# Three model blocks on one core: middle layers' projections as three fp32r products, attention outputs as halves three heads later, constants multiplied in TensorE's waits

## The reference, cut to what matters

```python
# second block, layer 0                       # layer 1
x = x + 0.5 * swiglu(rms_norm(x), ...)         # the same
proj = rms_norm(x) @ ab_w_in    # 1024x1536    # proj = rms_norm(x) @ c_w_in  (q k v 3072, index 512+64+8)
y = cat(pool_mixer(u), conv_module(a, gate))   # y = dsa_attention(...): 16 heads of 64
x = x + y @ ab_w_out            # 1024x1024    # x = x + y @ c_w_out
x = x + 0.5 * swiglu(rms_norm(x), ...)         # the same
# third block: swiglu, layer_norm; then
proj = h @ w_in ; y_ssm = mamba2_branch(z, xbc, dt) @ w_ssm_out
y_att = moba_attention(q, k, v) @ w_att_out    # 8 heads of 128
x = layer_norm(a*h + (g_ssm * y_ssm + g_att * y_att) @ w_o) ; then swiglu, layer_norm
```

## Time and profile before

| what | us |
|---|---|
| median of 3 executions | 3916.43 |
| the profiled execution | 3912.03 |
| its span, first to last instruction | 3910.2 |
| TensorE busy in it | 3252.5 (83%) |
| VectorE busy | 2156.8 (55%) |
| ScalarE busy | 1014.4 (26%) |
| mean granted TensorE clock | 0.952 of full |

### The profile page before, as it was taken

How to read it: one execution, slowest core, us unless ns; L and a number is a source line. 1 busy time by engine, 2 the same in 40 slices (tenths; PEclk the granted TensorE clock), 3 DMA queues, 4 the chain that set the end, 5 groups by cost and what they waited for, 6 DMA issues and landing times. The chain is left out here.

```text
span 3910.2 us, 34931 instructions
## 1 busy us (share of the span) xinstructions
PE 3252.5 (83%) x12416; PEld 2229.5 (57%) x12416; DVE 2156.8 (55%) x3737; ACT 1014.4 (26%) x1597; POOL 1033.1 (26%) x1092
## 2 busy tenths in 40 slices
PE   5897567778887577777998999999998989878798
PEld 3673222223664222223876687876687878767686
DVE  5578766544559766645544455523445435555654
ACT  0211111111112111112432344412343312434333
POOL 0027777764016777764000000000000000200000
PEclk9799899999899899999998999998999989989999
DMA  9369999999549999999651455542455534243453
GB/s 365 142 226 368 409 409 409 409 404 369 229 152 344 409 409 409 409 409 338 195 167 65 157 187 168 187 146 86 130 185 173 185 124 147 75 154 128 151 183 118
DMA packets 402041, 951.19 MB, mean 243 GB/s; under 512 B 30652, under 2 KB 171488, under 8 KB 401632
## 3 DMA queue, kind: packets, MB, share of 16 engines
q0 software_dynamic: 147456, 536.94, 34.9%
q1 hardware_dynamic: 245088, 397.09, 30.3%
q10 hardware_dynamic: 9344, 15.22, 1.1%
HBM read 948.06 MB, written 1.07 MB: 243 GB/s over the span
## 5 line engine op out<-in xcount | busy, mean ns | idle before, releaser
L1463 PE MATMUL PS<-v_rows,xn 128*128 128x512 f32 x1944 | 910.4, 612 | 360.9 <-DMA v_rows<-in_peer_v_dram,peer_ids 350.8
L1463 PEld LDWEIGHTS PS<-v_rows,xn 128*128 128x128 f32 x1944 | 356.4, 193 | 913.8 <-issue 553.6
L1544 DVE CUSTOM_DVE_ANT_0 u_rows<-u_rows,PS 128x1024 f32<-128x1024 f32 x512 | 621.8, 1220 | 365.9 <-DMA u_rows<-in_peer_u_dram,peer_ids 338.1
L760 DVE TENSOR_TENSOR ring_lo<-ring,ring_hi 128x2048 fp32r<-128x2048 f32 x198 | 452.9, 2292 | 260.3 <-ACT ring_hi L699 259.8
L1618 POOL DMA_INDIRECT u_rows<-in_peer_u_dram,peer_ids x512 | 484.7, 947 | 268.9 <-issue 145.2
L1618 POOL DMA_INDIRECT v_rows<-in_peer_v_dram,peer_ids x512 | 487.5, 952 | 169.3 <-issue 144.3
L699 ACT CAST ring_hi<-ring 128x2048 fp32r<-128x2048 f32 x198 | 376.7, 1912 | 287.1 <-PE PS L616 156.2
L616 PE MATMUL PS<-ring_hi,hT_hi 128*128 128x512 f32 x1056 | 420.2, 398 | 16.6 <-DVE hT_lo L800 12.1
L616 PE MATMUL PS<-ring_hi,hT_lo 128*128 128x512 f32 x1056 | 414.3, 392 | 0.0
L616 PE MATMUL PS<-ring_lo,hT_hi 128*128 128x512 f32 x1056 | 413.8, 392 | 0.0
L442 PE MATMUL PS<-hT,ring 128*128 128x256 f32 x1664 | 366.9, 382 | 1.2 <-DVE hT L406 1.2
(11 more groups left out here) (400 smaller groups left out, 3708.3 us busy)
## 6 DMA issues: line engine op xcount, KB each, us to landing
ring<-in_ffn_w_gate_dram SPq DMA_DIRECT2D x132, 512.0 KB, 3.9
ring<-in_ffn_w_up_dram SPq DMA_DIRECT2D x132, 512.0 KB, 4.9
ring<-in_ffn_w_down_dram SPq DMA_DIRECT2D x66, 1024.0 KB, 4.8
ring<-in_w_in_dram SPq DMA_DIRECT2D x64, 1024.0 KB, 5.1
ada_ring<-in_ada_w_dram SPq DMA_DIRECT2D x96, 512.0 KB, 8.6
ring<-in_peer_wq_dram SPq DMA_DIRECT2D x16, 1024.0 KB, 7.3
ring<-in_c_w_in_dram SPq DMA_DIRECT2D x14, 1024.0 KB, 5.0
ring<-in_w_out_dram SPq DMA_DIRECT2D x8, 1024.0 KB, 12.2
```

What stands on the lines that cost most here:

```text
L760: nc.vector.tensor_tensor(halves(c)[1], slot, halves(c)[0], ALU.subtract).then_inc(S.w_lo, 1)
L1463: ins = nc.tensor.matmul(self.PS[:, 2 * b + h, :], diag[:, r % NDIAG, :], rowsV[:, m % VRING, h * BANK:(h + 1) * BANK], start=(n % (slots ...
L1544: ins = nc.vector.tensor_tensor_reduce(rowsU[:, m % URING, :], rowsU[:, m % URING, :], H[b], 1.0, 0.0, ALU.mult, ALU.add, dots[:, e:e + 1])
```

## The change

1. `ab_in`, `ab_out`, `c_in` (but for its narrow job) and `c_out` go through `project_halves`. New `tokens_hi` and `tokens_lo` split `hT`; `self.plain` names chunks that aren't split; `output_projection` takes halves and the number of chunks prepared by the stage before.
2. Kind "F" is three products of 256 columns in every place; outputs lie in two banks, and the additions behind the old form (L2447 and L2478, and their like for the keys) go away.
3. `attention` writes its output as halves: ScalarE rounds head h-2 after it has copied the transposed weights of head h, VectorE subtracts head h-3 at the beginning of its step h. The later split in `att_out` goes away.
4. `norm_vector` does what it had between (a `weights_lo`) ahead of the wait for GpSimd's power.
5. `keep_clock` multiplies two constant 128x128 tiles into a PSUM bank that nobody reads, `count` times, at 28 places of the code.

```diff
+    def keep_clock(self, bank, count):
+        for _ in range(count):
+            self.nc.tensor.matmul(self.PS[:, bank, 0:P], self.ones, self.ident, start=True, stop=True, skip_group_check=True)
-    def norm_tensor(self, pe, S, src=None):
+    def norm_tensor(self, pe, S, src=None, lead=17, pause=4):
+        self.keep_clock(2, lead)
...
+        self.keep_clock(2, pause)
@@ norm_vector
         nc.vector.drain().then_inc(S.n_ms, 1)
+        if between:
+            between()
         ve.wait_ge(S.n_rstd, 1)
...
-        if between:
-            between()
+    def tokens_hi(self, act, S, hh):
+        act.drain()
+        for g in range(2):
+            if g == 1:
+                act.wait_ge(S.n_hT, self.N_HT)
+            self.nc.scalar.copy(hh[:, 4 * g:4 * g + 4, 0, :], self.hT[:, 4 * g:4 * g + 4, :]).then_inc(S.h_hi, 1)
+    def tokens_lo(self, ve, S, hh):
+        ve.drain()
+        for g in range(2):
+            ve.wait_ge(S.h_hi, g + 1)
+            self.nc.vector.tensor_tensor(hh[:, 4 * g:4 * g + 4, 1, :], self.hT[:, 4 * g:4 * g + 4, :], hh[:, 4 * g:4 * g + 4, 0, :],
+                                         ALU.subtract).then_inc(S.h_lo, 1)
@@ project_halves, kind "F"
-                            out, col = self.PS[:, quad + t, :], slice(t * P, (t + 1) * P)
-                            nc.tensor.matmul(out, w_hi[:, kk, col], both[:, k, :], start=st, stop=False, skip_group_check=True)
-                            ins = nc.tensor.matmul(out[:, 0:SEQ], w_lo[:, kk, col], tok_hi[:, k, :], start=False, stop=sp,
+                            out, col = self.PS[:, pair + t // 2, (t % 2) * SEQ:(t % 2 + 1) * SEQ], slice(t * P, (t + 1) * P)
+                            nc.tensor.matmul(out, w_hi[:, kk, col], tok_hi[:, k, :], start=(st and t % 2 == 0), stop=False, skip_group_check=True)
+                            nc.tensor.matmul(out, w_hi[:, kk, col], tok_lo[:, k, :], start=False, stop=False, skip_group_check=True)
+                            ins = nc.tensor.matmul(out, w_lo[:, kk, col], tok_hi[:, k, :], start=False, stop=sp, skip_group_check=True)
@@ ab_in, tensor and vector
-                    self.norm_tensor(pe, S)
-                    pe.wait_ge(S.n_hT, self.N_HT)
-                    self.project(pe, S, [("F", 512)] * 3, self.hT, KT)
+                    self.norm_tensor(pe, S, lead=23, pause=11)
+                    self.project_halves(pe, S, ["F"] * 3, hh[:, :, 0, :], hh[:, :, 1, :], KT, ready=S.h_lo)
+                    self.keep_clock(7, 9)
...
+                    self.norm_vector(ve, S, gain, None, lambda: self.weights_lo(ve, S, 0, 1))
+                    self.tokens_lo(ve, S, hh)
+                    self.weights_lo(ve, S, 1, 2)
@@ attention, vector
+            def out_lo(h):
+                ve.wait_ge(S.a_hi, h + 1)
+                nc.vector.tensor_tensor(YT_lo[rows(h), h // per, :], self.PS[rows(h), 4 + h % 2, 0:SEQ], YT_hi[rows(h), h // per, :],
+                                        ALU.subtract).then_inc(S.a_out, 1)
...
             for h in range(heads):
+                if h >= 3:
+                    out_lo(h - 3)
                 if h + 2 < heads:
                     masked(h + 2)
                 normalised(h)
-                if h >= 2:
-                    self.attention_out(ve, S, nc.vector.tensor_copy, h - 2, rows, per, YT)
@@ attention, scalar
+            def out_hi(h):
+                act.wait_ge(S.a_val, h + 1)
+                nc.scalar.copy(YT_hi[rows(h), h // per, :], self.PS[rows(h), 4 + h % 2, 0:SEQ]).then_inc(S.a_hi, 1)
...
                     exponentials(h + 1)
                 turned(h)
+                if h >= 2:
+                    out_hi(h - 2)
@@ c_in, scalar
+                    self.weights_hi(act, S, 4, 8)
                     for h in range(8):
                         act.wait_ge(S.index, h + 1)
...
                     for j in (3, 5, 7):
+                        self.weights_hi(act, S, 2 * j + 2, 2 * j + 6 if j < 7 else 2 * j + 3)
                         self.leave(act, j)
@@ c_in, vector
+                    self.weights_lo(ve, S, 6, 8)
                     evacuate(2)
@@ conv stage, the new ends of scalar and vector
+                    for c in (0, 2):
+                        nc.scalar.copy(YT_hi[:, 4 + c:6 + c, :], YT[:, 4 + c:6 + c, :]).then_inc(S.y_hi, 1)
...
+                    for i, c in enumerate((slice(0, 4), slice(4, 6), slice(6, 8))):
+                        ve.wait_ge(S.y_hi, i + 1)
+                        nc.vector.tensor_tensor(YT_lo[:, c, :], YT[:, c, :], YT_hi[:, c, :], ALU.subtract)
```

More of the change, by code:

```diff
@@ L480, in project_halves @@
                 if n >= self.base + self.ahead:
-                    pe.wait_ge(S.w_lo, n - self.base - self.ahead + 1)
+                    pe.wait_ge(S.w_lo, self.halves_made(n))
+                if ready is not None and j == first:
+                    pe.wait_ge(ready, g + 1)
                 w_hi, w_lo = [ring[:, n % self.half_slots, :].rearrange("p (k n) -> p k n", k=4)
@@ L580, in _, with ffn @@
                 self.sum_columns(self.PS[:, 0, KT:2 * KT], 1).then_inc(S.columns, 1)
-    def ffn(self, name, gain=None, layer_norm=None):
+                self.keep_clock(1, 14)
+    def ffn(self, name, gain=None, layer_norm=None, after=4):
         nc = self.nc
@@ L1814, in _, with output_projection, attention @@
                     nc.gpsimd.tensor_tensor(self.rstd[:], self.ms[:], self.neghalf[:, 0:NB], ALU.pow).then_inc(S.c_rstd, 1)
-            self.output_projection("ab_out", YT)
-    def output_projection(self, name, YT):
-        with self.stage("p_free0 p_free1", name) as (block, S):
+            self.output_projection("ab_out", YT_hi, YT_lo, 2)
+    def output_projection(self, name, YT_hi, YT_lo, ahead):
+        self.ahead = ahead
+        with self.stage("p_free0 p_free1 w_hi w_lo", name) as (block, S):
             @block.tensor
             def _(pe):
-                self.project(pe, S, [("T", 512)] * 2, YT, KT)
+                self.project_halves(pe, S, ["T"] * 2, YT_hi, YT_lo, KT)
+            @block.scalar
+            def _(act):
+                self.weights_hi(act, S, self.ahead, 4)
             @block.vector
             def _(ve):
+                self.weights_lo(ve, S, self.ahead, 4)
                 self.plain_residual(ve, S)
-    def attention(self, block, S, ctx, heads, dh, QT, KT_, V, mask, bias, YT):
+    def attention(self, block, S, ctx, heads, dh, QT, KT_, V, mask, bias, YT_hi, YT_lo):
         nc = self.nc
@@ L1917, in _ @@
                 normalised(h)
-                if h >= 2:
-                    self.attention_out(ve, S, nc.vector.tensor_copy, h - 2, rows, per, YT)
-            for h in (heads - 2, heads - 1):
-                self.attention_out(ve, S, nc.vector.tensor_copy, h, rows, per, YT)
+            for h in range(heads - 3, heads):
+                out_lo(h)
         @block.scalar
@@ L1942, in _ @@
                 turned(h)
-    ATT = "a_scores a_masked a_max a_exp a_norm a_turn a_turned a_val a_out"
-    def attention_out(self, eng, S, copy, h, rows, per, YT):
-        eng.wait_ge(S.a_val, h + 1)
-        copy(YT[rows(h), h // per, :], self.PS[rows(h), 4 + h % 2, 0:SEQ]).then_inc(S.a_out, 1)
+                if h >= 2:
+                    out_hi(h - 2)
+            for h in (heads - 2, heads - 1):
+                out_hi(h)
+    ATT = "a_scores a_masked a_max a_exp a_norm a_turn a_turned a_val a_hi a_out"
     def sparse_attention(self):
@@ L2100, in _ @@
                     pe.wait_ge(side, 48)
-                self.attention(block, S, ctx, AH, 64, QT, KT_, V, mask[:], B, YT)
-            self.output_projection("c_out", YT)
+                self.attention(block, S, ctx, AH, 64, QT, KT_, V, mask[:], B, YT_hi, YT_lo)
+            self.output_projection("c_out", YT_hi, YT_lo, 1)
     def turn_plain(self, pe, S, src):
@@ L2401, in mamba @@
         self.place_halves(ctx, 2)
-        both = hh[:].rearrange("p k i n -> p k (i n)")
         YT_hi = self.sb("ssm_yT_hi", [P, 16, SEQ], F32R, ctx=ctx)
         YT_lo = self.sb("ssm_yT_lo", [P, 16, SEQ], F32R, ctx=ctx)
-        with ExitStack() as inner, self.stage("p_free0 p_free1 w_hi w_lo z z_used q_lo g_ms g_rstd g_y turned scaled out_hi out_lo", "ssm_z") as (block, S):
+        with ExitStack() as inner, self.stage("p_free0 p_free1 w_hi w_lo z z_used g_ms g_rstd g_y turned scaled out_hi out_lo", "ssm_z") as (block, S):
             Z = self.gate[:].rearrange("p i (b n) -> p i b n", b=NB)
@@ L2578, in moba @@
         pre = self.xn[:].rearrange("p i (b n) -> p i b n", b=NB)
-        YT_hi = self.sb("moba_yT_hi", [P, KT, SEQ], F32R, ctx=ctx)
-        YT_lo = self.sb("moba_yT_lo", [P, KT, SEQ], F32R, ctx=ctx)
-        with self.stage("p_free0 p_free1 w_hi w_lo y_hi y_lo pre sig", "att_out") as (block, S):
+        with self.stage("p_free0 p_free1 w_hi w_lo pre sig", "att_out") as (block, S):
             def gate(i):
```

197 lines of the change are left out of this document (123 added, 74 removed).

## The result

The changed kernel takes 3898.51 us (median of 8 runs, 3886.48 to 3907.61) against 3920.66 us (3915.93 to 3930.78, 8 runs) before: ratio 0.9939, 95% interval 0.9921 to 0.9958, some 22 us. I had forecast 78.7 and a range that ends at 3878. The direction was right and the size wrong by a factor of three and a half. The profiled execution took 3892.48 us.

What follows compares the result with a forecast made beforehand. Outside the peer stages TensorE was taken as the bound, by its products and by half-clock stretches after waits. -43.7 - 2 + 18.2 + 23.1 - 2.8 - 71.5 = -78.7 us from 3916.4 gave 3838, range 3808 to 3878.

Steps and rivals of the forecast that it cites:

- Part 1: Projections: products in halves make 8 F jobs and 6 T jobs shorter, -43.7 us; four old halves F jobs, -2.
- Part 2: Splitting tokens, weights and outputs ahead of the projections: free in steady state, but unhidden at starts and in c_in, +18.2 us.
- Part 3: Sparse and third-block attention: VectorE's subtraction waits on a new round trip through TensorE and ScalarE, +23.1 us.
- Rival B: Attention: no round trip, because VectorE's subtraction is early enough or waits where it idled anyway; 3815 us, chance 0.12.
- Rival C: Attentions stay at half clock, a head taking TensorE 5.1 us in place of 4.0; 3865 us, chance 0.12.
- Part 4: att_out: TensorE's wait behind the later split and the queries' additions are taken away, -2.8 us.
- Part 5: Constants in TensorE's waits: free at full clock, gaining half of TensorE's half-clock work where it is the bound, -71.5 us.
- the six smaller starts: Third block: constants at six smaller stage starts were to gain -10 us.
- The third block's rest: Third block outside its attention: forecast at -22.0 us.
- sticks: The two stick-breaking attentions: constants were to gain -18 us there, ScalarE then bounding a head.
- Rival D: Constants raise the clock in only half of the places; 3874 us, chance 0.13.
- Rival E: Slower: dummies run at half clock and come 0.22 us late for each of 833; 3992 us, chance 0.03.

Runs made afterwards that it cites:

- e1: The changed kernel with none of its constants multiplied, all else as changed: 4101.9 us, ratio 1.0043 to the kernel before.
- e3: The changed kernel without constants and with attention's subtraction for head h-3 moved behind normalising head h: 4070.2 us in one run.
- e4: The changed kernel with c_in's banks emptied before the next job's last chunk is rounded, and chunk 7 split between the ReLUs: 4031.7 us in one run.
- after: The changed kernel itself, in its first profiled execution: 3892.48 us; median 3898.51 us, ratio 0.9939 to the kernel before.
- e2: The changed kernel with attention's subtraction for head h-3 moved behind normalising head h, constants kept: 4024.1 us, ratio 0.9869 to the kernel before.
- f1: The changed kernel run again, unedited, in a later group: 3894.0 us, ratio 0.9933 to the kernel before.
- g1: f2 with 28 constants for 26 in the stick-breaking attention and 5 and 4 more behind its second and third heads' sums: 3847.5 us, ratio 0.9815.
- f2: The changed kernel with the edits of e2 and e4 together: 3848.0 us, ratio 0.9833 to the kernel before.
- g0: f2 run again, unedited, in a later group: 3853.7 us, ratio 0.9812 to the kernel before.
- g3: g1 with the first chunk's subtraction behind the tokens' scaling and 19 constants for 23 in ab_in and c_in: 3848.0 us, ratio 0.9805.

## Why the prediction was wrong, step by step

**The miss in two sums.** I was off by 56 us. By the ratios, the parts other than constants were to give -7.2 us and gave +17 (e1), 24 off; the constants were to give -71.5 and gave -41, 30 off. Parts 1 to 4 and the last paragraph are on the 24, part 5 is on the 30.

**Part 1, products: right in kind, F jobs mis-sized.** The T jobs came out to 0.2 us for the two. For the new F job I had two prices, 0.11 from the gap of two neighbouring starts in the earlier trace rows, and 0.119 from a stream in the earlier trace rows, and took the first. The second has the right size: 0.120, eight jobs at 0.9 us, +7.5. That may be chance, since its instructions are of another kind (plain float32, 128 columns). The next row of the same timeline of the kernel before would have said so:

```profile
3423.08 0.28 PE L497 MATMUL PS<-tokens_halves,weights_lo 128*128 128x256 f32 x1
3423.19 0.40 PE L496 MATMUL PS<-tokens_halves,weights_hi 128*128 128x512 f32 x1
```

One old pair (768 columns) takes 0.35 us, from 3422.84 to 3423.19. That is 0.32 us of columns at 2.4 GHz and 0.03 for two instructions. A gap of two starts, read to the hundredth, can't settle 0.11 or 0.12.

The Trainium skill, "TensorE: Matmul & The Clock Gate", section "Back-to-back issue gap", gives columns over 2.4 plus about 2.5 ns for an isolated matmul, a gap that counts no weight load; for 256 columns that makes an estimate of 109 ns. The measured 120, with a load for each product, is some 11 ns above it. The rule in its Part 3 that I weighed (loads overlap only between different row groups) is not borne out: 289 full-height loads of 0.19 us each lie under 288 products spaced by 0.120, and at most the 11 ns could be theirs.

**Part 2, splitting: the waits right, their consequence missed.** Bank waits 3.03 us (3), index +4.7 (3.8), the conv stage +2.8 in e3, without constants (2.8). But e4 puts the waits of the last five jobs at 11.5 us against the 6 forecast: each bank wait brings 3.4 us of products at half clock, and the index step 4.9 more. I had costed the clock for the constants and not for the waits that the change itself adds.

**Part 3, the round trip: right, and nearly right in size.** It was forecast at 23.1 us, and taking it out gave 26.3 with constants and 21 without. The wait was 1.57 where I had 1.35. The two attentions came out at 11.5 + 9.7 us against 8.3 + 5.3 because I had also credited constants with 9.5 us there: e1 to after they gave 0.9 in the sparse attention and nothing in the third block's, where the clock was at half for 13.7 us of the stage (the last window in the section on the result). VectorE's wait set the time of a head, so TensorE's clock hardly counted. Rival B (no round trip) is out, by e2. Rival C (half clock all through) didn't happen in the sparse attention, 0.92 over the stage.

**Part 4** came as forecast within 1 us: -2.1 in `att_out`'s first jobs.

**Part 5, constants: the step that failed.** I took half of TensorE's time at half clock as gain, place by place. For ten microseconds "at the six smaller starts" I had no row of a bound TensorE, and for 7.2 around `ssm_in` one of 10.6 us, which makes 5.3. The third block's rest brought 6.3 of 22.0. The runs put a number on the step: outside peers and sticks, constants remove 220 us of half clock (e1 to after) or 209 (e3 to e2), and the time falls by 40.1 and 40.2 (38.3 and 37.4 by the blocks' ends). That is 0.19 us per us of half clock, not 0.5. The traces say why for the larger part: of the 218 us between e1 and after TensorE was idle in 101, where a clock is worth nothing, and busy in 117, half of which would be 58. The remaining 18 or so lie where TensorE was busy and another engine set the pace, as VectorE did in the attentions, or were given back, as in the scan (+1.8); only these places are shown. In the sticks 18 were forecast and 11.1 came in this profile (12.3 by the block's end), and none in f1's, 6.5 us longer than before, where the clock fell behind the two open pauses. Rival D (constants raise the clock in half of the places), at 3874, is nearest in price but not in mechanism: the clock did rise, from 308 us at half to 88, and the time didn't follow. Rival E (constants late) was real in mechanism, 1.2 us at `mix_out`'s transposes and 1.4 at `ssm_z`, but faster work behind them paid for it: these stages are 0.3 to 0.5 us shorter than before.

**What e3 adds.** Without constants and with the trip repaired, the rest is 2367.5 us against 2368.1 before, though parts 1, 2 and 4 alone promise -30. Of that, 7.5 us are the F jobs' price and 5.5 the clock behind the waits of `c_in`. The remaining 17 stand beside 48 us more at half clock (270 against 222). The profiles show where: at half, in us before and in e3, `ab_in` 7 and 17, the conv stage 16 and 24, `c_in` 14 and 24, `ab_out` 4 and 6, `c_out` 0 and 3, `ssm_z` 19 and 26, `att_in` 7 and 12, mostly starts where split operands are now waited for. That the 17 us are the price of this clock is argued, not tried.

## What to carry to other kernels

Before a filler is credited with half of the half-clock time, ask at each place whether TensorE's work is what ends last there; here only a fifth came back, and in nearly half of that time TensorE had nothing to multiply. Where an instruction that waits for another engine is put ahead of independent work on an in-order engine, that work waits too: one moved line was worth 27 us, more than the whole change. And a new wait of TensorE can have two prices, the wait and the clock behind it: in `c_in` 6.06 us of waiting and 3.4 of clock.

## What the runs showed of the hardware

- An unbroken stretch of matmuls need not bring the clock back: f1 had 23.98 us busy in 24.00 at 0.50. The same work ran at 1.00 in g1, where most of the pauses ahead of it were filled (4.07 us busy of 4.60, against 2.61 of 4.70), but also in after and f2, where they were not.
- One kernel takes one course or the other from execution to execution: 97.3 or 114.9 us in the two sticks, and a spread of 16 to 21 us (after, f1, f2, g0). With the pauses filled it is 5 us in g3; in g1 it is 4 without, 22 with the one execution at a mean clock of 0.932.
- An fp32r matmul with its load costs its columns at 2.4 GHz plus 13 to 17 ns: 0.120 us for 256 columns (34.6 us for 288), 0.230 for 512 (22.1 us for 96).
